# Loading a turned copy of two small parameter blocks with the table, instead of by a transfer of its own

## The reference

```python
def compress(k, pos_emb, w1, w2):
    b, s, g, dh = k.shape
    nseg = s // CMP_STRIDE
    r = CMP_BLOCK // CMP_STRIDE
    nc = nseg - r + 1
    seg = k.reshape(b, nseg, CMP_STRIDE, g, dh)
    blocks = jnp.concatenate([seg[:, i:i + nc] for i in range(r)], axis=2)
    blocks = blocks + pos_emb[None, None, :, None, :]
    flat = blocks.transpose(0, 1, 3, 2, 4).reshape(b, nc, g, CMP_BLOCK * dh)
    return jax.nn.gelu(flat @ w1) @ w2
```

## Time and profile before

| | |
|---|---|
| median of 3 runs | 1559.35 us (1559.22 to 1561.53) |
| profiled execution, its own time | 1559.35 us |
| its span, first to last instruction | 1557.5 us |
| TensorE matmuls, weight loads | busy 1519.1 us, 1441.0 us |
| VectorE, ScalarE | busy 1173.5 us, 999.3 us |
| TensorE's granted clock, mean | 0.995 of full speed |
| DMA queue of the kernel | 35568 packets, 243.65 MB, 45.2% of 16 engines |

### The profile page before, as it was taken

One profiled execution on the slowest core, in us unless ns is written; L12 is line 12 of the kernel. 1 busy time (PEld: TensorE's weight loads), 2 busy tenths in 40 slices (PEclk: granted clock), 3 DMA queues, 4 the chain that ended last, 5 costly groups with the idle time before them and its releaser, 6 DMA issues.

```text
span 1557.5 us, 31058 instructions
## 1 busy us (share of the span) xinstructions
PE 1519.1 (98%) x13406; PEld 1441.0 (93%) x13406; DVE 1173.5 (75%) x1623; ACT 999.3 (64%) x1480; POOL 2.8 (0%) x10
## 2 busy tenths in 40 slices
PE   8999999999999999999999999999999997999998
PEld 7999999999989999999999988968999886899997
DVE  6899766777758799667777668886888577688864
ACT  7676854656546776765655546685777458677753
POOL 0000000000000000000000000000000000000000
PEclk9999999999999999999999999999999999999999
DMA  7423145555554432244655545402655543265551
GB/s 286 166 85 131 56 136 190 203 179 191 188 187 158 142 109 84 83 163 163 244 190 183 193 166 235 147 17 85 214 190 189 190 158 114 65 206 190 190 189 55
DMA packets 35704, 245.63 MB, mean 158 GB/s; under 512 B 4208, under 2 KB 4592, under 8 KB 6512
## 3 DMA queue, kind: packets, MB, share of 16 engines
q1 hardware_dynamic: 35568, 243.65, 45.2%
HBM read 242.58 MB, written 1.05 MB: 156 GB/s over the span
## 4 chain that ended last, share of the span: by engine, by line
PE 81%; DVE 12%; ACT 5%; issue 1%; DMA 1%; SPq 0%; DVEq 0%; ACTq 0%
PE PS L405 80%; DVE WL L1900 3%; DVE SB L1909 2%; DVE SB L1900 2%; DVE SA L1900 2%; ACT SB L1177 1%; ACT WH L1180 1%; PE PS L408 1%; DVE SB L2166 1%; DMA RAW<-w_in 1%; ACT SB L1180 0%; ACT SB L1837 0%; DVE SA L1909 0%; DVE SA L2068 0%; DMA X<-xt 0%
## 5 line engine op out<-in xcount | busy, mean ns | idle before, releaser
L405 PE MATMUL PS<-XH,WH 128*128 128x256 f32 (+1 forms) x2536 | 716.4, 282 | 10.2 <-DVE WL L1900 3.4
L405 PE MATMUL PS<-XL,WH 128*128 128x256 f32 (+1 forms) x2536 | 713.9, 281 | 0.0
L405 PE MATMUL PS<-XH,WL 128*128 128x256 f32 (+1 forms) x2536 | 713.4, 281 | 0.0
L1180 ACT CAST WH<-RAW 128x2048 fp32r<-128x2048 f32 (+1 forms) x229 | 427.1, 1866 | 331.6 <-PE PS L405 318.7
L1900 DVE TENSOR_TENSOR WL<-RAW,WH 128x2048 fp32r<-128x2048 f32 (+1 forms) x229 | 511.4, 2234 | 132.9 <-ACT WH L1180 128.9
L405 PEld LDWEIGHTS PS<-XH,WH 128*128 128x128 f32 (+1 forms) x2536 | 478.2, 189 | 17.9 <-issue 6.9
L405 PEld LDWEIGHTS PS<-XL,WH 128*128 128x128 f32 (+1 forms) x2536 | 476.4, 188 | 3.0 <-issue 2.4
L405 PEld LDWEIGHTS PS<-XH,WL 128*128 128x128 f32 (+1 forms) x2536 | 475.7, 188 | 0.3
L405 PE MATMUL PS<-INHL,WH 128*128 128x512 f32 (+1 forms) x1216 | 334.5, 344 | 1.2 <-DVE INHL L1900 1.2
L405 PE MATMUL PS<-INHL,WL 128*128 128x256 f32 x960 | 270.1, 281 | 0.0
L405 PEld LDWEIGHTS PS<-INHL,WH 128*128 128x128 f32 x1216 | 210.1, 188 | 29.0 <-ACT INHL L1180 1.5
(11 more groups left out here) (149 smaller groups left out, 1277.6 us busy)
## 6 DMA issues: line engine op xcount, KB each, us to landing
RAW<-w_in SPq DMA_DIRECT2D x51, 1024.0 KB, 4.9
RAW<-w_up SPq DMA_DIRECT2D x44, 1024.0 KB, 4.9
RAW<-f_in SPq DMA_DIRECT2D x44, 1024.0 KB, 4.9
RAW<-w_down SPq DMA_DIRECT2D x22, 1024.0 KB, 4.9
RAW<-f_out SPq DMA_DIRECT2D x22, 1024.0 KB, 4.9
RAW<-a_w_in SPq DMA_DIRECT2D x10, 1024.0 KB, 5.5
RAW<-w_out SPq DMA_DIRECT2D x8, 1024.0 KB, 4.9
RAW<-w_bdn SPq DMA_DIRECT2D x4, 1024.0 KB, 4.9
```

What stands on the lines that cost most here:

```text
L405: return e.matmul(out, l, r, start=start, stop=stop, skip_group_check=True)
L1180: e.copy(out, x).then_inc(*A.up(*key, of=of))
```

## The change

The turned copies become two more parts of the table, `pe_k_turned` and `pe_v_turned`, 16 columns each. The tile `PE2`, its transfer, its semaphore and VectorE's wait on it go. The table has 868 columns instead of 836.

```diff
@@ par_layout
-                    ("sinks", 16), ("pe_k", 16), ("pe_v", 16)]:
+                    ("sinks", 16), ("pe_k", 16), ("pe_v", 16),
+                    ("pe_k_turned", 16), ("pe_v_turned", 16)]:
@@ program
-        PE2 = sb("PE2", 32)
-        s_mv, s_pe2 = line("s_mv_loaded", 16), line("s_pe2_loaded", 16)
+        s_mv = line("s_mv_loaded", 16)
@@ vector, nsa, cmp_in
-                            pe = par(("pe_k", "pe_v")[n], 0, 16) if h == g % 2 else PE2[:, 16 * n:16 * n + 16]
-                            pe = pe.unsqueeze(2).to_broadcast([128, 16, 15])
+                            pe = par(("pe_k", "pe_v")[n] + ("" if h == g % 2 else "_turned"), 0, 16).unsqueeze(2).to_broadcast([128, 16, 15])
@@ vector, nsa
-                waits(V["angles", st], s_pe2["pe2"])
+                w.wait_ge(*V["angles", st])
@@ sync
                 if i == FIRST_CMP_LOAD:
-                    e.dma_start(PE2[:, :], a["pe2"]).then_inc(*s_pe2.up("pe2"))
                     for s in fence("f0", "f1"):
@@ layout
-        pe(cp[0]), pe(cp[1])], axis=1))
-    a["pe2"] = np.ascontiguousarray(np.roll(a["par"][:, -32:], 64, axis=0))
+        pe(cp[0]), pe(cp[1]), np.roll(pe(cp[0]), 64, axis=0), np.roll(pe(cp[1]), 64, axis=0)], axis=1))
```

## The result

The changed kernel takes 1569.34 us in the median of 4 runs (1568.25 to 1570.4), against 1560.44 us for the kernel before on the same chip (1559.22 to 1563.15). The ratio is 1.0054, with a 95% interval of 1.0037 to 1.0073: the change makes the kernel slower by some 9 us. The forecast was no change that can be measured, 1559.4 us, within 1557.4 to 1561.5.

A forecast was written before the change was run, and what follows sets the result against it. The prediction took TensorE's stream of matmuls to bound the kernel. To the span of 1557.5 us it added 0.04 for the larger table, all else 0, plus 1.85 around it: 1559.4 us, range 1557.4 to 1561.5.

The forecast's parts named there:

- the shift of addresses: Tiles from the table on move 128 bytes in each partition; matmuls at three places take 281 to 283 ns; term 0.
- The first paragraph of the prediction: Whole kernel: a stream of matmuls; a change touching none can only move TensorE's 38 us without work, or what feeds it.
- The rival: Matmuls on the low halves and feed-forward inputs: the 128-byte shift makes them slower, 4.7 us per nanosecond, 1564.1 us; chance 0.04.
- The signs of being wrong: Matmul groups with another mean, a start stall on table or fourth load, or TensorE's idle before compression no longer 2.6 us.
- The small load, removed: Second layer's feed-forward part: nobody waited for the 16 KB load, its reader had 177 us of slack; term 0.
- The larger table: Start of the kernel: 16 KB extra delay the fourth weight load's landing by 0.04 us, bounds 0 and 0.05.
- The wait and the adds: VectorE's position adds: removing the wait saves 0, at most 0.05 us; reading all from the table 0, at most 0.02.
- The fixed time of the small load: Rival: the load's fixed cost lay on the path and comes back, 1557.5 or at most 1554.7 us; chance 0.03.
- The sum: Whole kernel: 1557.5 + 0.04 - 0 - 0 = 1557.54 us of span, plus 1.85, makes 1559.4 us.

The follow-up runs named there:

- e1: The kernel before with an unused tile of 128 bytes a partition between the table and XL, nothing else changed: 1571.13 us, ratio 1.0059.
- e10: The kernel before with 32 unused bytes ahead of XL, one execution: 1583.39 us, against 1561.98 us for the kernel before.
- e4: The kernel before with 128 unused bytes ahead of all tiles, so that all move alike: ratio 1.0006.
- e2: The changed kernel with the turned values in a small tile behind all others, loaded at the start, every tile at its old address: ratio 1.0005.
- e8: The changed kernel with 128 unused bytes behind its table, XL 256 bytes further than in the kernel before: ratio 0.9999.
- e13: A kernel of TensorE alone, the same three matmuls on zeros at stepped distances of XL and XH: 340.1 to 363.2 ns for three in the values told.
- e15: TensorE alone on zeros, 256 placements of XH, XL and WL in shuffled order: most near 353.3, 356.7 or 360 ns for three matmuls, lowest 340.0.
- e18: e16 with 96 unused bytes directly ahead of the second work area and the feed-forward inputs: 1546.43 us, ratio 0.9906.
- e14: The kernel before with 128 unused bytes ahead of XH and 32 ahead of XL: 1562.64 us, against 1561.9 us before.
- e16: The changed kernel with tiles ordered WH, WL, RAW, PR, 32 unused bytes, XH, XL, C: 1548.23 us, ratio 0.9921.
- e5: The kernel before with 128 unused bytes between the constants and XH: ratio 1.0027.
- e6: The kernel before with the table placed ahead of XH, XL staying where it was: ratio 1.0047.

## Why the prediction was wrong, point by point

**The step that failed** is the one on the shift of addresses: "Three places, one duration. I take 0." The shift alone measured 9.6 us (e1: 1571.13 against 1561.53 us, ratio 1.0059). The first paragraph of the prediction has the same fault in general form: it says that a change that touches no matmul can only move the 38 us in which TensorE doesn't work, or what feeds it. This change touched no matmul and lengthened the other 1519 us. Two things were wrong in the step. It read the durations of matmuls, where the distance between starts makes the time; in the earlier trace rows the durations are 280 to 283 ns, while the starts of the same trace are 116.2 ns apart behind XH,WH and some 118.4 behind the other two kinds. Between runs the durations do move, but not in the measure of the time: in e10, which is 21 us slower, they are 284 to 286 ns. And it took three tiles at fixed places as three samples of an address, while e4 shows that the address is harmless: what counts is how the tiles that TensorE reads lie to each other. XH, XL and the feed-forward inputs were each timed at one distance to the weights only, and no row of one trace could show what another distance does.

**The rival was the right mechanism,** the shift of 128 bytes making matmuls slower, and its chance of 0.04 was too low: all that stood against it were the equal durations. Its price was of the right kind: "One nanosecond in the distance between two of them makes 4.7 us". Measured over all 2512 triples, disturbed ones and gaps included, were 3.6 ns for three matmuls, 9.1 us (the undisturbed rows have 4.2 ns), and 1.1 ns on 960 of the feed-forward inputs, 1.1 us. Its place was half right: not the moving operand as such, but where XL lies to XH and the weights.

**The signs of being wrong.** Of the three that the prediction named, one showed: a matmul group has a different mean, XH,WH with 286 ns for 283. It is the group whose input did not move; the group on the low halves, which the prediction expected at 282, has 281. The other two, a stall at the start and another idle time before the compression's matmuls, did not show, and TensorE's idle time stayed near 38 us.

**The small load, removed: 0.** Held. e2 has no transfer in the middle and is at 1.0005 of the time; e8, which is the whole change with XL well placed, is at 0.9999; e1 keeps the transfer and is as slow as the changed kernel. The load behind it in the queue waited for its slot as before.

**The larger table: 0.04 us.** The fourth weight chunk landed at 21.53 us, where it was 21.43: 0.10 us later instead of 0.04, and as little to be measured in the whole. e8 has the larger table too, and its ratio of 0.9999 (0.9990 to 1.0008) leaves room for no more than 1.6 us either way.

**The wait and the adds: 0.** Held: TensorE's idle time until the adds are through is 2.5 us, where it was 2.6, and all sixteen take 571 ns in the median:

```profile
L1900 DVE TENSOR_TENSOR SA<-SB,PR x16: 551/571/584, 955.9 to 964.9; 64x240 f32<-64x240 f32 x16
```

**The fixed time of the small load, and the rule on coalescing.** The change is what the rule of the Trainium skill asks for ("DMA: Bandwidth & Descriptors", section "Rules for kernel authors"). The 1.9 to 4.7 us that the rows show are off the path, and e2 and e8 show that they don't come back. The figure of about 2 us, which the prediction took from the section "Anatomy of one DMA" of the same page of the Trainium skill, is given there for transfers that GpSimd issues; the two loads here are SyncE's, so their own rows are the better source.

**The sum** was right, as far as the runs can tell, in every term but one, and that one was the only term that touched all 2512 triples. A term of 0 on the engine that is busy for 98% of the time needs better evidence than any other.

## What to carry to other kernels

A tile made wider moves every tile behind it. Where TensorE is the bound, compare the number of matmuls in a full window before and after (here 342 against 338 in 40 us) rather than their durations, and if it differs, put unused bytes in front of the moved tiles before looking for a wait. Which distances are good can be measured with TensorE alone in one run, but should then be tried in the kernel, since the stream can have more than one level at the same distances.

## What the runs showed of the hardware that was not expected

With no other engine at work and the full granted clock, a matmul of 128x256 in this stream starts 113.4 to 121 ns after the one before, according to where the weights and the two inputs lie to each other within 256 bytes (e13, e15; two of the 256 stretches of e15 took longer). In the kernel that makes 1546 to 1583 us (e18 to e10) with the same matmuls. The Trainium skill, in "TensorE: Matmul & The Clock Gate", section "Step-by-step: what each phase is for", says that TensorE has two read ports and that loading the next tile's weights takes no read bandwidth from the running matmul. The measurements don't agree as far as the step between two matmuls goes: moving the inputs against the weights, with their own distance kept, took the three matmuls from 362.4 to 352.9 ns (e10, e14), and TensorE alone took 360 or 363 ns at the first of these placements and 353 or 354 at the second, in three stretches each. They do not show which of the reads is held up.

The same distances give more than one level, 340 or 353 ns in e16 to e18, 351 or 360 in e5 and 352 or 360 in e6, each kept over a whole feed-forward part. What picks the level was not found. A placement that takes the fast one throughout would be worth, as an estimate, at most 13 ns on each of 2512 triples, 33 us; the best that was measured, e18, has 15.5 us of it (1546.43 against 1561.95 us).
